# Sixteen expert slots, four fillers moved into the scan's hole, expert weights of the second matrix in 8 KB rows, and the first expert pass taken out of its loop

## The reference

```python
h_lat, h_ctx = modulate(rms_norm(x, g), ...), modulate(rms_norm(ctx, g), ...)   # 256 + 256 tokens
p = h @ w_in                       # GDN q,k,v | z | beta, a | GLA q,k,v | r | low-rank gate | branch gates
o_a = gated delta rule on GDN heads (8 x 128), both directions, chunked, with a triangular solve
o_b = gated linear attention (4 heads), both directions
y = sigmoid(gates_a) * (norm(o_a) * silu(z) @ w_out_a) + sigmoid(gates_b) * (norm(o_b) * silu(r) @ w_out_b)
x = x + g1 * (y @ w_out)
h = modulate(rms_norm(x, norm_ffn_g), ...)
top 4 of 32 experts per token, softmax weights p:
  gu = h @ w_gu[e] + b_gu[e];  act = min(glu, 7) * sigmoid(1.702 * glu) * (clip(lin, -7, 7) + 1)
  x = x + g2 * sum_e p_e * (act @ w_down[e] + b_down[e])
```

## Time and profile before

| | us |
|---|---|
| median of 3 runs | 2121.72 |
| lowest and highest | 2120.38, 2124.76 |
| the profiled execution | 2120.16 |
| its span, first to last instruction | 2118.1 |
| busy PE, DVE, ACT, POOL in it | 1920.5, 614.9, 435.6, 66.9 |
| mean granted clock of TensorE | 0.976 |

### The profile page before, as it was taken

The page is one execution under the profiler, slowest core; times in us unless marked ns, Lnnn a source line. Parts: engine busy times, 40 slices in busy tenths (PEclk is TensorE's granted clock), DMA queues, the critical chain, the costliest instruction groups (busy, mean ns, idle before and its releaser), DMA issues. The chain is left out here.

```text
span 2118.1 us, 24891 instructions
## 1 busy us (share of the span) xinstructions
PE 1920.5 (91%) x9336; PEld 1037.7 (49%) x9336; DVE 614.9 (29%) x1347; ACT 435.6 (21%) x870; POOL 66.9 (3%) x86
## 2 busy tenths in 40 slices
PE   6999996999999789999999888989998889999997
PEld 3346454978878443323333333233333244767775
DVE  1476464438320311101111111111111122532223
ACT  3222731346311121001111110111111022521011
POOL 1000500100000000000000000000000000000000
PEclk9999997899999999999999999999999999999999
DMA  8443347134544579999999999999999971214442
GB/s 357 159 172 139 143 113 152 61 113 139 191 162 156 238 289 416 419 419 419 416 418 416 418 416 419 419 420 417 417 417 417 397 262 68 96 50 149 153 158 105
DMA packets 140187, 566.73 MB, mean 268 GB/s; under 512 B 35904, under 2 KB 43840, under 8 KB 100736
## 3 DMA queue, kind: packets, MB, share of 16 engines
q1 hardware_dynamic: 140128, 565.92, 68.7%
HBM read 555.26 MB, written 10.62 MB: 267 GB/s over the span
## 5 line engine op out<-in xcount | busy, mean ns | idle before, releaser
L2026 PE MATMUL expert_gb<-expert_ring,hT 128*64 128x512 f32 x1024 | 270.5, 607 | 69.8 <-DMA expert_ring<-in_w_gu 68.2
L2026 PE MATMUL expert_lb<-expert_ring,hT 128*64 128x512 f32 x1024 | 262.8, 592 | 0.0
L1931 DVE TENSOR_SCALAR hT<-expert_gb 128x512 f32<-128x512 f32 x32 | 22.1, 692 | 717.7 <-PE expert_lb L2026 717.7
L2074 PE MATMUL expert_yb<-expert_ring,hT 128*64 128x512 f32 x512 | 222.7, 592 | 1.5 <-DMA expert_ring<-in_w_down 1.5
L2074 PE MATMUL expert_yb<-expert_ring,h2T 128*64 128x512 f32 x512 | 222.8, 592 | 0.0
L2026 PEld LDWEIGHTS expert_gb<-expert_ring,hT 128*64 128x64 f32 x1024 | 59.3, 135 | 250.5 <-DMA expert_ring<-in_w_gu 201.1
L467 PE MATMUL mix_in_pj<-hT,mix_in_pj_ring 128*128 128x512 f32 (+1 forms) x384 | 144.5, 536 | 1.3 <-DVE hT L587 1.3
L2026 PEld LDWEIGHTS expert_lb<-expert_ring,hT 128*64 128x64 f32 x1024 | 72.8, 137 | 147.0 <-issue 147.0
L2424 PE MATMUL attend_bank<-hT,expert_ring 128*128 128x256 f32 x640 | 141.4, 379 | 0.0
L2074 PEld LDWEIGHTS expert_yb<-expert_ring,hT 128*64 128x64 f32 x512 | 69.9, 137 | 143.3 <-issue 140.4
L2424 PEld LDWEIGHTS attend_bank<-hT,expert_ring 128*128 128x128 f32 x640 | 121.6, 190 | 25.1 <-issue 9.6
(11 more groups left out here) (468 smaller groups left out, 2266.1 us busy)
## 6 DMA issues: line engine op xcount, KB each, us to landing
expert_ring<-in_w_gu SPq DMA_DIRECT2D x256, 1024.0 KB, 19.7
expert_ring<-in_w_down SPq DMA_DIRECT2D x128, 1024.0 KB, 20.7
fill_w<-in_w_fill SPq DMA_DIRECT2D x48, 512.0 KB, 3.8
mix_in_wm<-in_w_mod_units SPq DMA_DIRECT2D x11, 2048.0 KB, 9.0
expert_ring<-in_w_up_units SPq DMA_DIRECT2D x22, 1024.0 KB, 5.5
mix_in_pj_ring<-in_w_in_units SPq DMA_DIRECT2D x12, 1024.0 KB, 4.8
expert_ring<-in_w_down SPq DMA_DIRECT2D x22, 512.0 KB, 3.4
expert_ring<-in_w_in SPq DMA_DIRECT2D x4, 2048.0 KB, 11.7
```

The lines of the kernel that those rows point to most:

```text
L1931: v.tensor_scalar(glu, gb[j][:], LIMIT, None, ALU.min).then_inc(s_glu, 1)
L2026: m = pe.matmul(b[halves[h], :], xT[:, k, x], ring[:, z, c0 + 512 * h:c0 + 512 * h + 512], start=False, stop=(k == KT - 1))
L2074: m = pe.matmul(yb[h][halves[j], :], hidT[j][:, c, hh * SLOTS:(hh + 1) * SLOTS], ring[:, z, a * F + 512 * h:a * F + 512 * h + 512], start= ...
```

## The change

- `FILL_AT` becomes scan 2 to 19, linear 20 to 35, merge 36 to 47. PE runs fillers 6 to 17 during the inversion, 18 and 19 where 14 and 15 were. From filler 10 to 17, ACT issues the store of its own copy and the load two ahead; SP keeps the rest. Four results of branch gates are so written to DRAM (`NPARKED`) and read back in merge with the load of the second half of `pz`, which grows from 1 to 1.5 MB.
- The ring has 16 slots: twelve as before, two in a new tile `late` (in merge `ra` and `rb`, in the second layer `wuq` and `gpost2`), one in `ob`, one in the fillers' weight buffer. In merge 16 units are loaded ahead. The bias picks get a small tile of their own (96 x 64), and GpSimd makes its copies from them by broadcast.
- A pair has 24 units and the ring 16 slots, so SP's and PE's loops take two pairs per turn, in which each unit has a fixed slot.
- `w_down` is laid out on the host so that a unit has 8 KB in a row for each partition.
- The first pass is written ahead of the loop, with p = 0; the count is asked for before each engine's last stretch of it, and one comparison jumps over the other passes. The first pass uses `posp` as merge left it, without the subtraction.

```diff
-EXPERT_RING = 12
+EXPERT_RING = 16
+EXPERT_UNITS = 24
+NPARKED = 4
-FILL_AT = {"mix_in": (0, 2), "delta_scan": (2, 16), "linear": (16, 32), "merge": (32, FILL)}
+FILL_AT = {"mix_in": (0, 2), "delta_scan": (2, 20), "linear": (20, 36), "merge": (36, FILL)}
...
-                for f in range(F0, F1):
+                for f in range(F0, 12):
                     if f >= F0 + 2:
                         S.fill.store(sp, f - 2)
-                    S.fill.load(sp, f + 2)
+                    if f < 10:
+                        S.fill.load(sp, f + 2)
...
+                for f in range(F1 - 2, F1):
+                    S.fill.store(sp, f)
+                    S.fill.load(sp, f + 2)
                 for d in d2:
                     copied(sp, ("y6", d, NTILE - 1))
...
-                for f in range(F1 - 2, F1):
-                    S.fill.store(sp, f)
                 S.fill.all_stored(sp, F1)
...
-                for f in range(6, 14):
+                for f in range(6, 18):
                     copy_fill(f)
+                    if f >= 10:
+                        S.fill.store(act, f)
+                        S.fill.load(act, f + 2)
...
-                for f in range(6, 14):
+                for f in range(6, 18):
                     fill(f)
...
-        ra, rb = s.sb("ra", [P, HA, L]), s.sb("rb", [P, HB, L])
+        ra, rb = (S.late[:, n, :].rearrange("p (k n) -> p k n", n=L)[:, 0:k] for n, k in ((0, HA), (1, HB)))
...
-                sp.dma_start(pz[:, HA:2 * HA], A.fill_latent[HB + HA:HB + 2 * HA].rearrange("c p n -> p c n")).then_inc(s_in, 16)
+                sp.dma_start(pz[:, HA:2 * HA + NPARKED], A.fill_latent[HB + HA:].rearrange("c p n -> p c n")).then_inc(s_in, 16)
...
+                sp.dma_start(S.pick[:], A.bias_pick).then_inc(s_tab, 16)
                 sp.wait_ge(S.fill.done, F1)
-                sp.dma_start(S.pick, A.bias_pick).then_inc(s_tab, 16)
+                load_expert_unit(sp, A, S, 0, 15, 15)
                 sp.wait_ge(s_pa, 2)
+                load_expert_unit(sp, A, S, 0, 14, 14)
                 for n in range(8, 12):
-                    load_expert_unit(sp, A, S, 0, n)
+                    load_expert_unit(sp, A, S, 0, n, n)
                 sp.wait_ge(s_y, 1)
                 for n in range(4):
-                    load_expert_unit(sp, A, S, 0, n)
+                    load_expert_unit(sp, A, S, 0, n, n)
                 sp.wait_ge(s_t, 4)
-                for n in range(4, 8):
-                    load_expert_unit(sp, A, S, 0, n)
+                for n in (4, 5, 6, 7, 12):
+                    load_expert_unit(sp, A, S, 0, n, n)
+                sp.wait_ge(s_xs, 2)
+                load_expert_unit(sp, A, S, 0, 13, 13)
...
+def load_expert_unit(sp, A, S, pair, u, z):
+
+    dst = S.unit[z]
...
-        src = A.w_down[bass.ds(e, 1), 2 * n * P:2 * (n + 1) * P, :].rearrange("e (a p) n -> p (e a) n", p=P)
-        dst = dst.rearrange("p (a n) -> p a n", a=2)
+        src = A.w_down_units[bass.ds(e, 1), n].rearrange("e p n -> (e p) n")
     sp.dma_start(dst, src).then_inc(S.landed[z], 16)
...
+            known = []
+
+            def ask():
+
+                if not known:
+                    known.append(eng.value_load(S.count[0:1, 0:1], min_val=0, max_val=L))
+
+            body(0, ask)
+            with eng.If(known[0] > SLOTS):
+                with eng.Fori(1, L // SLOTS) as p:
+                    with eng.If(known[0] > p * SLOTS):
+                        body(p, ask)
...
+                    with sp.Fori(0, PAIRS // 2 - 1) as i:
+                        for n in range(RING, RING + 2 * PER):
+                            sp.wait_ge(s_used, (p * PAIRS + i * 2) * PER + (n + 1))
+                            load_expert_unit(sp, A, S, i * 2 + n // PER, n % PER, n % RING)
+                    for n in range(RING, 2 * PER):
+                        sp.wait_ge(s_used, p * (PAIRS * PER) + ((PAIRS - 2) * PER + n + 1))
+                        load_expert_unit(sp, A, S, PAIRS - 2 + n // PER, n % PER, n % RING)
...
+                    with pe.Fori(0, PAIRS // 2 - 1) as i:
+                        it = p * PAIRS + i * 2
+                        middle(it, 0, True)
+                        ups(it + 1, 1)
+                        spread(it)
+                        middle(it + 1, 1, True)
+                        ups(it + 2, 0)
+                        spread(it + 1)
+                    ask()
+                    middle(first + (PAIRS - 2), 0, True)
+                    ups(first + (PAIRS - 1), 1)
+                    spread(first + (PAIRS - 2))
+                    middle(first + (PAIRS - 1), 1, False)
                     spread(first + (PAIRS - 1))
...
+            S.late = mix.sb("late", [P, 2, 2 * D])
+            S.unit = [S.ring[:, z, :] for z in range(12)] + [S.late[:, 0, :], S.late[:, 1, :], S.ob[:].rearrange("p k n -> p (k n)"),
+                                                           S.fill.w[:].rearrange("p a k n -> p (a k n)")]
+            S.pick = mix.sb("bias_pick", [3 * NE, 2 * NE])
```

More of the change, by code:

```diff
@@ L1802, in _ @@
                 v.tensor_copy(S.count[:], most[:])
-def load_expert_unit(sp, A, S, pair, u):
-    z = u % EXPERT_RING
-    dst = S.ring[:, z, :]
+def load_expert_unit(sp, A, S, pair, u, z):
+    dst = S.unit[z]
     if u < 2 * KT:
@@ L1820, in expert_stage @@
     RING = EXPERT_RING
-    PER = 2 * RING
+    PER = EXPERT_UNITS
     PAIRS = NE // 2
@@ L1837, in expert_stage @@
         xb = [b[:].rearrange("p (k n) -> p k n", k=4) for b in (gb[0], lb[0])]
-        landed, ring = S.landed, S.ring
+        landed, unit = S.landed, S.unit
         (s_used, s_sel, s_gx, s_xT, s_selw, s_pt, s_put, s_glu, s_lin, s_sig, s_hid, s_tr, s_trc,
@@ L1852, in passes @@
         def passes(eng, body):
-            count = eng.value_load(S.count[0:1, 0:1], min_val=0, max_val=L)
-            with eng.Fori(0, L // SLOTS) as p:
-                with eng.If(count > p * SLOTS):
-                    body(p)
+            known = []
[7 more added lines that the diff above has]
+                        body(p, ask)
         with nc.Block() as block:
@@ L1889, in _, with body @@
                 g.sem_inc(s_pt, 1)
-                def body(p):
+                def body(p, ask):
+                    ask()
                     with g.Fori(0, PAIRS) as i:
@@ L1942, in hidden, with body @@
                     between(3)
-                def body(p):
-                    v.tensor_scalar(S.posp[:], S.pos[:], shift[:, bass.ds(p, 1)], None, ALU.subtract).then_inc(s_shift, 1)
-                    v.wait_ge(s_shift, p + 1)
+                def body(p, ask):
+                    if not isinstance(p, int):
+                        v.tensor_scalar(S.posp[:], S.pos[:], shift[:, bass.ds(p, 1)], None, ALU.subtract).then_inc(s_shift, 1)
+                        v.wait_ge(s_shift, p)
                     first = p * PAIRS
@@ L2009, in gather, with slot, arrived, ups @@
                     m.then_inc(s_gx, 1)
-                def ups(it):
+                def slot(n, odd):
+                    return (PER * odd + n) % RING
+                def arrived(it, n, odd):
+                    return it * PER + (16 * ((PER // 3 * odd + n) // RING + 1) - PER // 3 * odd)
+                def ups(it, odd):
                     pe.wait_ge(s_xT, it + 1)
@@ L2021, in ups @@
                             u = j * KT + k
-                            z = u % RING
-                            pe.wait_ge(landed[z], it * 32 + 16 * (u // RING + 1))
+                            z = slot(u, odd)
+                            pe.wait_ge(landed[z], arrived(it, u, odd))
                             for b, c0 in ((gb[j], 0), (lb[j], F)):
@@ L2040, in spread, with middle @@
                                   start=True, stop=True).then_inc(s_sc, 1)
-                def middle(it, more):
+                def middle(it, odd, more):
                     for j in range(2):
@@ L2066, in middle @@
                             u = 2 * KT + 2 * n + j
-                            pe.wait_ge(landed[u % RING], it * 32 + 16 * (u // RING + 1))
+                            pe.wait_ge(landed[slot(u, odd)], arrived(it, u, odd))
                         for a in range(2):
@@ L2072, in middle @@
                                 for j in range(2):
-                                    z = (2 * KT + 2 * n + j) % RING
+                                    z = slot(2 * KT + 2 * n + j, odd)
                                     m = pe.matmul(yb[h][halves[j], :], hidT[j][:, c, hh * SLOTS:(hh + 1) * SLOTS],
-                                                  ring[:, z, a * F + 512 * h:a * F + 512 * h + 512],
+                                                  unit[z][:, a * F + 512 * h:a * F + 512 * h + 512],
                                                   start=False, stop=(f == 7))
@@ L2929, in tables @@
     rope = np.stack([np.cos(ang), np.sin(ang)]).reshape(2, 2, P, ROPE // 2).transpose(2, 0, 1, 3)
-    pb = np.zeros((3 * NE, NE, SLOTS), np.float32)
-    for e in range(NE):
```

(4 more changed lines are left out.)

73 lines of the change are left out of this document (33 added, 40 removed).

## The result

The changed kernel takes 2104.89 us (median of 4 runs, 2098.72 to 2106.16), the kernel before 2122.35 beside it: ratio 0.9912, 95% interval 0.9895 to 0.9928. It is faster by 17.5 us. The forecast was 2086.7, 35.0 us less, with a range of 2078 to 2098; the time lies 6.9 us above the range. Two later sets of the changed kernel gave 2104.07 and 2101.97 (ratios 0.9920 and 0.9897); the median of all 13 runs is 2104.3, and they scatter from 2098.7 to 2111.0.

A forecast was written before the change was run, and what follows sets the result against it. The prediction took the expert stage as bound by weight transfers, with a chain through PE, DVE and ACT ahead of it. Terms summed to -35.0 us from 2120.16, 2085.2; with 1.56 for the median, 2086.7, range 2078 to 2098.

The forecast's parts named there:

- Fillers in merge: Merge: four fillers leave PE's path, 14.58 us off, less 1.4 for reading their results back; net -13.2 us.
- the parked read: Merge: four results read back from DRAM, 0.52 MB more in the load ACT's Silu waits for; +1.4 us, bounds 0 and 3.5.
- Fillers in the scan: Delta scan: four fillers run in PE's 15.65 us hole; +2.5 us late, -2.5 us clock, net 0, bounds -6 and +6.
- the sign of a wrong scan: Delta scan: a y6 group, after the scan's last filler, later than 390 would show the scan forecast wrong.
- The held-up rival: Scan: ACT's loads and the block gathers delay each other, second group 5 us later, clock low again; 2091.7 us, chance 0.12.
- The clock rival: Scan: half-speed fillers and the small matmuls between them run at 2.4 GHz; 7 us less, 2079.7 us, chance 0.17.
- Ring of sixteen: Expert stream: sixteen units loaded ahead in merge leave 368 instead of 372; -9.95 us, bounds 0 and 10.2.
- rows of 8 KB: Expert stream: down units in longer rows move at 421 instead of 410 GB/s; -9.1 us, bounds 0 and -9.1.
- the other two prices in the prediction: Down weights' longer rows by the Trainium skill: worth nothing (sum 2095.8), or 3.7 us by fixed packet cost (sum 2092.1).
- become the bound: Expert stage: PE needs at most 55.7 us a pair against 59.7 for transfers, so it stays 4 us ahead.
- Entry and exit: First expert pass outside the loop: less DVE idle at both boundaries; entry -1.54 us, exit -1.2, bounds 0 and -1.6.

The follow-up runs named there:

- scan_back: The changed kernel with the four fillers back in merge and the scan as before; 2105.9 us.
- scan_back5: Second run of the changed kernel with the four fillers back in merge and the scan as before; 2103.91 us, beside the changed kernel at 2101.97.
- entry_loop: The changed kernel with the first expert pass back in the loop, with value load and subtraction; 2106.27 us.
- again: The changed kernel, unaltered, run for a second profile; 2104.07 us.
- between: The changed kernel with early filler weight loads, fitted idle-time matmuls, and filler 18 between the two y5 groups; 2087.35 us, ratio 0.9831.

## Why the forecast was wrong

**Fillers in merge** (-13.2): right in size. The traces gave -14.0, -12.6 and -12.4 against before, -14.1 against scan_back. The Silu came 1.7 us later where +1.4 stood for the parked read; as it came 1.8 and 0.5 us later in scan_back and scan_back5 without that read, the +1.4 may be right by luck.

**Fillers in the scan** (net 0, bounds -6 and +6): this step failed. Its words were "two or three loads of 0.5 MB fall between them: 0 to 4 us later, I take 2", and "-2.5 us clock". The part put down to the clock came near, -2.0 us behind the second group. The lateness was the term that failed: the second group came 8.7 us late where +2.5 stood, 7.7 of it in the gathers, with four loads and their stores beside them. The stretch grew by 6.7, 6.8 and 9.2 us, outside its bound of +6, and y6 began at 397.35, past the 390 that the prediction had named as the sign of a wrong scan. Two errors made it. I counted the loads of the fillers that move, of which two fall into the gathers, and left out those of fillers 18 and 19, which ACT issues in the same loop. And I let the pacing of SP's issue hide part of the transfer, though the DMA engines were busy already during the gathers. The window of the kernel before (PE busy, clock, DMA share, GB/s) shows it, 157 GB/s at a share of 1.52:

```profile
345.00:350.00 5.00, 0.00 (x0) 0.50 1.52 157
```

The held-up rival was the right mechanism, priced at 5 where the second group lost 8.7. Its chance of 0.12 was too low, given that the Trainium skill's rule quoted there and the 2.70 us wait both pointed that way. The clock rival was priced wrongly too: of the 7.9 us that the clock could give back, 2.5 were in the sum already, so 5.4 were left and not 7.

**Ring of sixteen and rows of 8 KB** (-9.95 and -9.1): nearly right. A pair takes 59.66 us where 59.7 was forecast, the rows measured 8.6 to 9.7, where the other two prices in the prediction were 0 and 3.7, and PE did not become the bound (57.2 us of waits left). The 2.487 us a unit in the sum fit the measured 60.26 us a pair; by the 421 GB/s named beside them it would be 2.491, and the rows' term -8.6. The stream's stretch with the exit fell by 17.2 and 18.3 instead of 20.3: 1.5 and 1.3 of that is the exit, and the cause of the rest, 1.5 and 0.6 us, is open.

**Entry and exit** (-1.54 and -1.2): from DVE's last instruction in merge to the picks it is 1.57 us less (the idle fell from 2.22 to 0.94, and the subtraction is gone), but the low clock over the gather and the first units, put at nothing, cost 2.3 to 2.5 (2.7 to 2.9 against entry_loop), more than the entry gave. The exit brought +0.3 and +0.1 and not -1.2; of the bounds "0 and -1.6" the wrong side was open.

**What I had not priced**: the router at half clock in this execution (+3.1), the earlier clock (+2.95 at the inversion's end), and the second layer's (+2.1; again has +0.5). I read these as where the clock falls, not as the change, since other profiles with the same code lack them; again, with a lucky router and an unlucky start, came out 2.9 us below the profiled execution. Summed from the forecast's own -35.0: scan +6.7, start +2.95, stream and exit +3.0, second layer +2.1, router and entry +6.1 (2.09 + 2.46 + 1.54), the stretch ahead of merge +0.2, merge -0.8: -14.8, the difference of the two spans (the executions differ by 15.1).

What stays open: whether the move of the fillers alone made the kernel faster than scan_back (6.2 by rows, 0.8 by medians), what the Silu's later data comes from, what else than the loads holds the gathers (2.7 us), and the exit's 5.03 us.

## What to carry to other kernels

A hole in which an engine waits for small DRAM round trips is not free for work that brings its own loads: count every load and store issued inside the hole, by whatever engine, and add the loads' bytes at the full rate to the round trip; the small stores seem to cost more than that. Load ahead into memory that is dead until later: that brought 12.3 us of median here, 9 to 12 of them in the scan, though a wait of 3.76 us for the second block stayed. And when a stretch is bound by the stream, it did not matter where four slots were filled ahead of it, as long as the DMA engines were idle there.

## What the runs showed of the hardware

- Rows of 4 KB and of 8 KB per partition don't stream alike: 418 and 422 GB/s over the same 700 us, 60.28 and 59.66 us a pair, and 410 and 422 where down units land. The Trainium skill's 512 B for line rate (DMA: Bandwidth & Descriptors, Specifications) does not hold at the percent level here.
- The low clock moves with small shifts of PE's idle time. With 1.57 us taken out of a wait, half clock lay over the first units in eight profiles of eight, and in neither of two without; filling a 3.76 us wait left the low behind it (label between). Matmuls that compute nothing, 29 fitted into waits, took it away over the first units: 4.5 us of a stretch, by one profile.
- The exit behind loops whose body had doubled on PE and SP left DVE 5.03 us idle in one profile, against 2.54 before; the cause is not isolated.
